# Experts' rows of a two-block network: the selection step ahead of the diagonal, one operation a step

## The reference

```python
def peer(h, w_query, sub_keys, u_tab, v_tab):          # blocks of P = 128 tokens
    qry = (xb @ w_query).reshape(P, 8, 2, 128)
    s = jnp.einsum('phcd,hckd->phck', qry, sub_keys)   # 16 x 128 scores a token
    top_s, top_i = lax.top_k(s, 16)
    cand_s = top_s[..., 0, :, None] + top_s[..., 1, None, :]      # 8 x 256 pairs
    cand_i = top_i[..., 0, :, None] * 128 + top_i[..., 1, None, :]
    best_s, pos = lax.top_k(cand_s, 16)
    idx = jnp.take_along_axis(cand_i, pos, axis=-1)    # 8 x 16 = 128 experts a token
    gate = jax.nn.softmax(best_s, axis=-1)
    act = jax.nn.gelu(jnp.einsum('pd,phkd->phk', xb, u_tab[idx]), approximate=False)
    return jnp.einsum('phk,phkd->pd', gate * act, v_tab[idx])
```

## Time and profile before

| | us |
|---|---|
| median of three runs | 4776.7 |
| lowest and highest | 4774.76, 4783.31 |
| profiled execution | 4781.35 |
| its span, first to last instruction | 4779.6 |

### The profile page before, as it was taken

One profiled execution on the slowest core, in us unless ns is written; L12 is line 12 of the kernel. 1 busy time (PEld: TensorE's weight loads), 2 busy tenths in 40 slices (PEclk: granted clock), 3 DMA queues, 4 the chain that ended last, 5 costly groups with the idle time before them and its releaser, 6 DMA issues.

```text
span 4779.6 us, 42366 instructions
## 1 busy us (share of the span) xinstructions
PE 3826.1 (80%) x13554; PEld 2124.1 (44%) x13554; DVE 3151.6 (66%) x6481; ACT 708.2 (15%) x1677; POOL 1257.2 (26%) x1210
## 2 busy tenths in 40 slices
PE   7879879998788888778797987776887768677776
PEld 3434438543476767668553542222222236222222
DVE  3756537486567677664788668878766445787666
ACT  1231110035211111111101110010100021100000
POOL 0001000010133433320243433433543100334433
PEclk9789889999798989888899999999999889899999
DMA  5424136434100000005598999899999611898998
GB/s 205 163 97 156 45 145 240 189 112 163 67 7 23 5 23 21 9 5 203 205 415 331 403 409 386 334 401 350 385 422 421 251 53 45 334 387 345 418 421 357
DMA packets 139856, 1069.57 MB, mean 224 GB/s; under 512 B 15472, under 2 KB 15856, under 8 KB 21488
## 3 DMA queue, kind: packets, MB, share of 16 engines
q0 software_dynamic: 112320, 817.94, 42.7%
q1 hardware_dynamic: 27312, 248.92, 13.6%
HBM read 1056.31 MB, written 10.49 MB: 223 GB/s over the span
## 4 chain that ended last, share of the span: by engine, by line
PE 38%; DVE 36%; issue 9%; DMA 8%; POOL 5%; ACT 3%; DVEq 0%; POOLq 0%; SPq 0%; ACTq 0%
PE bank L199 18%; DVE arena L2802 9%; DMA arena<-in_uv,arena 6%; PE bank L2759 5%; POOL arena L2784 4%; DVE arena L2807 3%; ACT arena L211 3%; DVE arena L217 3%; DVE arena L221 2%; PE bank L2074 2%; DVE arena L440 2%; PE bank L2344 2%; DVE arena L547 2%; PE bank L1597 2%; PE bank L2082 1%
## 5 line engine op out<-in xcount | busy, mean ns | idle before, releaser
L2759 PE MATMUL bank<-arena 128*128 128x512 f32 x3072 | 1529.6, 628 | 486.7 <-DVE arena L2807 485.3
L199 PE MATMUL bank<-arena 128*128 128x128 f32 (+5 forms) x4896 | 1303.1, 425 | 78.9 <-DMA arena<-in_w_mod 16.2
L2784 POOL DMA_INDIRECT arena<-in_uv,arena x768 | 838.7, 1092 | 1438.2 <-PE bank L2759 890.6
L2759 PEld LDWEIGHTS bank<-arena 128*128 128x128 f32 x3072 | 544.4, 193 | 1450.4 <-DVE arena L2807 929.1
L2802 DVE CUSTOM_DVE_ANT_0 arena<-arena 128x1024 f32<-128x1024 f32 x768 | 942.0, 1227 | 297.1 <-DMA arena<-in_uv,arena 233.0
L199 PEld LDWEIGHTS bank<-arena 128*128 128x128 f32 (+3 forms) x4896 | 815.2, 196 | 556.2 <-issue 435.3
L211 ACT ACTIVATE arena<-arena 128x1 f32<-128x1 f32 (+8 forms) x1025 | 311.8, 304 | 2742.9 <-DVE arena L2802 1895.8
L2807 DVE TENSOR_SCALAR arena<-arena 128x128 f32<-128x128 f32 x768 | 300.2, 391 | 233.9 <-ACT arena L211 219.8
L211 ACT ACTIVATE arena<-bank 128x512 f32<-128x512 f32 (+3 forms) x464 | 248.2, 535 | 1166.5 <-PE bank L2061 528.9
L2144 POOL TENSOR_TENSOR arena<-arena 128x512 f32<-128x512 f32 x128 | 164.4, 1285 | 450.8 <-PE bank L2074 445.6
L440 DVE CUSTOM_DVE_ANT_0 arena<-arena 128x1024 f32<-128x1024 f32 x192 | 240.8, 1254 | 31.8 <-DMA arena<-in_w_rows 19.3
(11 more groups left out here) (252 smaller groups left out, 2829.4 us busy)
## 6 DMA issues: line engine op xcount, KB each, us to landing
arena<-in_w_rows SPq DMA_DIRECT2D x52, 1024.0 KB, 4.9
arena<-in_w_in SPq DMA_DIRECT2D x16, 2048.0 KB, 7.9
arena<-in_dn_w SPq DMA_DIRECT2D x12, 2048.0 KB, 9.3
arena<-in_wq SPq DMA_DIRECT2D x12, 2048.0 KB, 8.4
arena<-in_w_up SPq DMA_DIRECT2D x11, 2048.0 KB, 8.9
arena<-in_dn_wo SPq DMA_DIRECT2D x8, 2048.0 KB, 11.1
arena<-in_w_rows POOLq DMA_DIRECT2D x12, 1024.0 KB, 5.1
arena<-in_uv,arena POOLq DMA_INDIRECT x768, 12.1
```

Source lines behind the costliest of these rows:

```text
L199: t = p.e.matmul(out, l, r, start=(i == 0), stop=(i == n - 1))
L2759: t = p.e.matmul(by[half], m["dg"][ee % 4], m["uv"][r][:, 1024 + 512 * half:1536 + 512 * half], start=(ee == 0), stop=(ee == 127))
L2784: g.e.indirect_dma_start(out=m["uv"][q % 7], out_offset=None, in_=self.I["uv"], in_offset=bass.IndirectOffsetOnAxis(ap=m["idx"][n % 2][:, ...
```

## The change

Four edits. The step of the selection is taken between a row's dot product and its diagonal instead of behind the diagonal. Each of the eight steps that look up expert numbers becomes three steps of one operation. The last step is cut in two, with two `yield`s between the request for the exponential and the wait for it. The 17 last late steps come every 4 rows instead of 5, so their last is at row 140, row 12 of the second tile, and selection there starts at row 14. `SELECT` is 99 instead of 83: the indices are made at row 107 instead of 91 of a tile, and at 113 in the second tile as before.

```diff
-                + [(10 + 8 * 6 + 18 + 5 * j, 17 + j) for j in range(17)])
+                + [(10 + 8 * 6 + 18 + 4 * j, 17 + j) for j in range(17)])
...
-    SELECT = 16 * 3 + 1 + 2 + 8 * 3 + 2 * 4
+    SELECT = 16 * 3 + 1 + 2 + 8 * 3 + 8 * 3
...
                 v().tensor_tensor(c4[:, hh], bc(m["posf"][:, c, hh], 3, 16), iof[:, hh], ALU.is_equal
                                   ).then_inc(*V.up(k + ".i"))
+                yield
                 v().tensor_tensor(c4[:, hh], c4[:, hh], bc(i8[:, hh, c, :], 2, 16), ALU.mult).then_inc(*V.up(k + ".i"))
+                yield
                 red(v, ij[:, c, hh], c4[:, hh], ALU.add).then_inc(*V.up(k + ".i"))
                 yield
...
         v().tensor_tensor(g3, best, bc(best[:, :, 0], 2, 16), ALU.subtract).then_inc(*V.up(k + ".g", n))
+        yield
+        yield
         v.wait_ge(*A.of(k + ".g", n))
...
                                          m["acts"][:, ee:ee + 1]).then_inc(*V.up(k + ".dot", n, ee))
+                if ee >= self.select_row(m["layer"], n):
+                    next(ahead, None)
                 v.wait_ge(*A.of(k + ".act", n, ee))
                 if q > 3:
                     v.wait_ge(*P.of(k + ".y", *divmod(q - 4, 128)))
                 v().tensor_scalar(m["dg"][ee % 4], self.ident, m["coef"][n % 2][:, ee:ee + 1],
                                   m["gates"][n % 2][:, ee:ee + 1], ALU.mult, ALU.mult).then_inc(*V.up(k + ".dg", n, ee))
-                if ee >= self.select_row(m["layer"], n):
-                    next(ahead, None)
                 self.late_step(n, ee, late)
```

## The result

The changed kernel takes 4709.2 us, median of four runs (4707.7 to 4712.3), against 4775.7 us of the kernel before on the same chip: a ratio of 0.986, with a 95% interval of 0.984 to 0.988. Predicted were 4677 us, with a range of 4650 to 4716. The sign and the range hold; of the 99 us that the sum gave, 67 came. The spread of the range upward stood for a first tile that loses and for diagonals that meet the issue; neither brought most of what is missing, so that 4709 lies inside it is in part luck. The profiled execution spans 4708.7 us, 70.9 less than the one of before. Of that, 2.7 us lie ahead of the experts' first row, where nothing was changed.

The account below looks back on a forecast made before the run. VectorE was taken to bound the selecting tiles and TensorE layer 0's first; afterwards the gather. Gains of 1, 4.5, 0, 31.6, 29.7 and 31.4 make 98, plus 1 for exponential waits: 4776.7 - 99, about 4677 us (4650 to 4716).

Parts of the forecast that it names:

- a first tile that loses: Rival: in layer 0's first tile, weights waited for by 10 us at each change, -20 there; 4698 us, chance 0.10.
- diagonals that meet the issue: Rival: diagonals collide with GpSimd's gather issue, 0.23 us a row over 98 rows, VectorE bounds again; 4739 us, chance 0.11.
- the rival that the gap isn't filled (4744): Rival: the step starts no sooner than the gelu's end, only the splitting gains, 33 us in all; chance 0.05.
- 0.235 us a row: Selecting rows: VectorE time saved by moving the step into the 0.27 us idle between dot and diagonal.
- VectorE's need of 290: Layer 1's tile, rows 9 to 127: VectorE's time after the change, 290 us, against the gather's 296.5.
- the gather becomes the bound of the whole tile: Layer 1's tile: after the change the gather's need exceeds VectorE's by some 6 us, so it sets the pace.
- 2.513 us: The gather's pace per row, interruptions included, taken from the two tiles where nothing is selected.
- The rival that selection slows them (4797): Rival: VectorE's denser steps slow the gathers in rows 9 to 106, at 2.85 us a row; chance 0.03.
- the estimate from 358 GB/s: All tiles: from the Trainium skill's HBM-to-core rate, a row would take an estimated 2.93 us and every tile lose.
- 175 us: TensorE's time from the first tile's row 83 to the second's row 12, against 174.0 before; no gain taken.
- my own mark (waits for the weights past 10 us): Sign that the prediction is wrong: TensorE's waits for the query weights passing 10 us.
- the 0.76 us: Row 8: the first step's time, won because its wait for the scores is covered by the diagonal's gelu wait.

Follow-up runs that it names:

- the own wait gone: Changed kernel, diagonal not waiting for VectorE's own step, the wait for the matmul of four rows before moved ahead of the dot: 4683.1 us; without that move 4685.0.
- a spacing that fits the load: Changed kernel with the last late steps 3, 3, 3 and 7 rows apart instead of every 4 rows: 4689.5 us.
- seven diagonals: Changed kernel without the diagonal's own-step wait, late steps 3, 3, 3, 7 rows apart, seven diagonal buffers instead of four, no wait for the earlier matmul: 4662.7 us.

## Why the prediction was right, and where it was 32 us off

**Bound and mechanism.** VectorE bounded the selecting tiles and TensorE the first; each shortened as far as VectorE's rows did. The order alone gave 42 us and splitting gave about 9 a full tile, so the rival that the gap isn't filled (4744) is out: steps start 1.27 us after the dot.

**The step that failed: 0.235 us a row.** I took 1.50 - 1.27 and left the step's distance to the diagonal at 0.03 us, that of two operations of one step. It is 0.14. The rows had a warning: the 0.14 us ahead of every dot, which I used for the dot alone. The saving is 0.13 us, as the run of the order alone and the run with the order undone both show. Put into my own sum for layer 1's tile (rows 9 to 127), VectorE's need of 290 becomes 290 + 98 x 0.105 = 300.3 us; measured are 116.6 + 73.5 + 24.4 + 86.0 = 300.5. That is above the gathers' 296.5, so the sentence "the gather becomes the bound of the whole tile" fell with it. In the three full tiles it cost 23 of the 32 us: 92.7 predicted, 69.5 measured. With the own wait gone, VectorE drops below the gathers, and the tiles win 89.8.

**The gathers' pace.** I took 2.513 us; where they bound rows under selection they ran at 2.480, and the tile at 421 GB/s. The rival that selection slows them (4797) is refuted by the same stretch, and so, for this case, is the estimate from 358 GB/s. The 392 GB/s of the earlier trace rows were VectorE's pace.

**The first tile.** Up to row 83 the gain is 4.8 us where 5.5 were expected. Behind it I had 175 us and measured are 180.3. The weights' waits are 15.1 instead of 13.2, mostly by the third (4.73 instead of 3); the slow groups 6.8 for my 7; the end 5.05 as taken. The remaining 3 us are TensorE's as well. I had counted one broadcast and there are two (L566), 1.8 us. And for this tile's end I put in TensorE's idle alone, where I took 6.9 for the others: behind it a row's four matmuls take 3.75 us instead of 1.98 and the next group 4.61 instead of 3.62, 2.8 together. TensorE does about half a row less in the stretch than the 58 I took, so it adds up to within half a microsecond. By my own mark (waits for the weights past 10 us) their sum was a warning, though none alone passed 5.2. The rival by which this tile loses 20 had the right sign and too large a size. The fault is in what I set the 175 us beside: the 174.0 of before hold 2.5 groups of query matmuls fewer, 8.7 us at 3.46 each, and 16.4 us in which TensorE waited for VectorE. The new pace filled that time with work and waits for weights. By its own run the 4-row pace costs 12.6 us, which the other parts of the change pay back in this tile but for 2.8. Five rows wouldn't do with 99 steps in the second tile; a spacing that fits the load was worth 20.

**Row 8, the closing step, the diagonals.** Row 8 won 0.7 us of the 0.76. The diagonals are 0.35 us in all 99 selecting rows of the third tile (8 to 106); before, 18 of these rows had 0.58, 13 of them in plain rows behind the selection. In the changed kernel only plain rows have 0.58, behind the selection as the earlier trace rows had it, and rows 4 to 7. GpSimd's issues in selecting rows fall beside step and diagonal, 0.94 us in nearly all, and not into the dot:

```profile
3314.30 0.94 POOL L2788 DMA_INDIRECT arena<-in_uv,arena  x1 [1.64 <-DVE arena L2724]
...
3375.94 1.92 POOL L2788 DMA_INDIRECT arena<-in_uv,arena  x1 [0.31 <-DVE arena L2813]
```

The first is in a selecting row, the second in a plain one behind it. The rival in which diagonal and issue meet (4739) didn't occur.

**Still open:** whether seven diagonals are worth anything in the time itself, and what the closing step's cut is worth alone.

## What to carry to other kernels

When an operation is moved into another's wait, price both of its new borders, each by a row in which the same kinds of waits meet; 0.1 us a border was nearly half of what the filled gap should give here. A wait for the engine's own last instruction is worth leaving out where nothing of that instruction is read: one such wait a row was 24 to 26 us here. Steps that share a load should be spaced by the load and not evenly: dense while the weights are there, and the whole pause where the next ones have to come.

## What the runs showed of the hardware

- A VectorE diagonal that doesn't wait for the step before it starts 0.08 us ahead of that one's recorded end; with the wait and one or two other semaphores beside, 0.11 or 0.14 us behind it. With the own wait alone, between operations of a step, it is 0.03. A dot behind a diagonal starts a little later: 0.14 us with one other semaphore, 0.17 with two.
- A wait instruction without the own semaphore passes beside the running operation and costs nothing (0.01 us after the operation's start in the records).
- A pause of TensorE of 5 us costs another 1.8 to 2.6 us in the 16 matmuls behind it (5.41 to 6.20 us instead of 3.62), with the granted clock at 0.93 in the stretch instead of 1.00. In the first of these groups the clock is 0.50, the lower of its two levels, from 2613.6 to 2616.0 us, and 1.00 again from 2619.5 on.
- The gathers' pace of 2.48 us, of undisturbed plain rows before, is the same with a selection step in each of 99 rows: 421 GB/s over the 118 rows from row 9 on.
